# Places of all expert picks made once, eight row buffers, and a third of layer 1's modulations moved ahead of the one-hot vectors

## The reference, cut to what matters

```python
sc = einsum('thsd,hskd->thsk', q, subkeys)      # 8 heads, 2 sides, 128 keys
sv, si = top_k(sc, 16)
best, ci = top_k(sv[:, :, 0, :, None] + sv[:, :, 1, None, :], 16)
idx = i1 * 128 + i2                             # 8 * 16 = 128 picks for each token
act = gelu(x @ u_tab[idx])                      # one number for each pick
out = sum over picks of softmax(best) * act * v_tab[idx]    # rows of 1024
m = silu(c) @ w_mod[layer] + b_mod[layer]       # 48 tiles of 128 modulations
```

## Time and profile before

| | us |
|---|---|
| median of 3 runs (5010.95 to 5015.53) | 5015.15 |
| the profiled execution: its own time | 5005.07 |
| its span in the trace | 5003.3 |
| ACT starts behind layer 0's last input product | 1599.86 |
| the same in layer 1 | 4150.47 |

### The profile page before, as it was taken

One profiled execution on the slowest core, in us unless ns is written; L12 is line 12 of the kernel. 1 busy time (PEld: TensorE's weight loads), 2 busy tenths in 40 slices (PEclk: granted clock), 3 DMA queues, 4 the chain that ended last, 5 costly groups with the idle time before them and its releaser, 6 DMA issues. The chain is left out here.

```text
span 5003.3 us, 77426 instructions
## 1 busy us (share of the span) xinstructions
PE 4526.0 (90%) x27516; PEld 4053.8 (81%) x27516; DVE 3145.1 (63%) x6219; ACT 1177.7 (24%) x1696; POOL 2654.9 (53%) x1462
## 2 busy tenths in 40 slices
PE   7789999999999888888869889999999998999997
PEld 6768999999998666666658679999999997777775
DVE  6962498199994666566643431992799973444444
ACT  2052111132322222222222431110232322222221
POOL 3403455444443777777752124555444436888885
PEclk9889999999999999999988999999999999999998
DMA  5401244377677666666621011444577676666773
GB/s 203 149 9 60 84 120 120 109 154 159 155 162 202 234 244 239 250 236 250 240 76 35 26 47 64 119 119 122 124 159 162 153 172 237 249 251 252 250 253 131
DMA packets 823649, 797.66 MB, mean 159 GB/s; under 512 B 566513, under 2 KB 601041, under 8 KB 822898
## 3 DMA queue, kind: packets, MB, share of 16 engines
q1 hardware_dynamic: 175248, 500.38, 29.8%
q10 hardware_dynamic: 603106, 159.70, 14.8%
q0 software_dynamic: 45056, 134.38, 7.7%
HBM read 640.41 MB, written 153.89 MB: 159 GB/s over the span
## 5 line engine op out<-in xcount | busy, mean ns | idle before, releaser
L498 PE MATMUL acc<-a_hi,w_hi 128*128 128x320 f32 x5296 | 1671.5, 316 | 45.8 <-DVE a_lo L1270 32.3
L500 PE MATMUL acc<-a_hi,w_lo 128*128 128x320 f32 x5296 | 1641.9, 310 | 0.1
L499 PE MATMUL acc<-a_lo,w_hi 128*128 128x320 f32 x5296 | 1641.5, 310 | 0.0
L498 PEld LDWEIGHTS acc<-a_hi,w_hi 128*128 128x128 f32 x5296 | 1000.5, 189 | 51.2 <-issue 35.1
L499 PEld LDWEIGHTS acc<-a_lo,w_hi 128*128 128x128 f32 x5296 | 1001.1, 189 | 1.4 <-issue 0.2
L500 PEld LDWEIGHTS acc<-a_hi,w_lo 128*128 128x128 f32 x5296 | 999.2, 189 | 0.4 <-issue 0.4
L420 POOL TENSOR_TENSOR w_lo<-w_in,w_hi 128x1024 fp32r<-128x1024 f32 (+1 forms) x345 | 891.7, 2585 | 27.7
L436 POOL CAST w_hi<-w_in 128x1024 fp32r<-128x1024 f32 x256 | 306.4, 1197 | 1060.9 <-DMA w_in<-in_u 1060.9
L464 POOL TENSOR_TENSOR w_lo<-w_in,w_hi 128x1024 fp32r<-128x1024 f32 x256 | 698.7, 2729 | 53.8 <-ACT w_hi L1096 49.0
L741 PE MATMUL aux<-p_his,w_hi 128*128 128x512 f32 x1024 | 445.4, 435 | 272.0 <-POOL w_lo L464 149.5
L1505 DVE SCALAR_TENSOR_TENSOR one_b<-iota_b,picks_t 128x384 bf16<-128x384 bf16 x1024 | 633.5, 619 | 0.0
(11 more groups left out here) (244 smaller groups left out, 6265.5 us busy)
## 6 DMA issues: line engine op xcount, KB each, us to landing
w_in<-in_u SPq DMA_DIRECT2D x256, 512.0 KB, 4.0
w_in<-in_v SPq DMA_DIRECT2D x256, 512.0 KB, 5.9
gate_s<-gates ACTq DMA_DIRECT2D x64, 1024.0 KB, 14.0
ag<-act_s SPq DMA_DIRECT2D x256, 256.0 KB, 4.7
ag<-gate_s SPq DMA_DIRECT2D x256, 256.0 KB, 5.3
act_s<-a_out ACTq DMA_DIRECT2D x184, 256.0 KB, 3.6
w_mod_v<-in_w_mod SPq DMA_DIRECT2D x48, 512.0 KB, 3.6
act_s<-tmp ACTq DMA_DIRECT2D x72, 256.0 KB, 3.6
```

What stands on the lines that cost most here:

```text
L498: pe.matmul(out, wh, hi[:, k, n], start=(k == 0), stop=False)
L499: pe.matmul(out, wh, lo[:, k, n], start=False, stop=False)
L500: return pe.matmul(out, wl, hi[:, k, n], start=False, stop=(k == kt - 1))
```

## The change

**Places.** `next_where` is gone. After routing, one cast makes the places of all 128 picks (`where_i`), and POOL waits for them once in each layer. **Buffers.** `found` has eight row buffers; the fetch of row k waits until pick k-8 has been added. The activations land in `pick_act`, a column for each pick, so no fetch of one waits for DVE. POOL's value loop is written out. **Start of the stage.** POOL issues eight row fetches before its first `w_lo`, makes `w_lo` of six chunks, and only then waits for all stored activations (`a_st`) and issues eight activation fetches; before, this wait stood behind the first `w_lo`. From chunk 8 on it issues one row and one activation for each chunk, as before. **Products.** `form` multiplies in place in `ag`, so SP's load of `ag` for chunk n waits for `p_lo` of chunk n-4; SP's order of `ag` and v is swapped, and so is ACT's order of `high_p` and `high_v`. **Modulations.** 16 of the 48 tiles are computed on DVE in layer 0 between the end of the routing (`shifted`) and the exponent, their weights loaded by SP beside the input chunks 48 to 55; the loop computes two tiles for each eight chunks, not three. **Exponent.** ACT takes it eight chunks earlier, in both layers.

```diff
+        MODS_U = 16
+        MODS_AT = range(6 * SPLIT, 7 * SPLIT)
@@ SP
+                if l == 0:
+                    with sp.Fori(0, MODS_AT.start // SPLIT) as i:
+                        for u in range(SPLIT):
+                            load_inputs(u + SPLIT * i, u)
+                    sp.wait_ge(shifted, 1)
+                    for c in MODS_AT:
+                        load_inputs(c, c % SPLIT)
+                        for t in (2 * (c - MODS_AT.start), 2 * (c - MODS_AT.start) + 1):
+                            if t >= 4:
+                                sp.wait_ge(mod_u_used, t - 3)
+                            sp.dma_start(w_mod_u[:, t % 4, :], a["w_mod"][1, t]).then_inc(mod_u_in[t % 4], 16)
...
-                        sp.wait_ge(p_made, NKEY * l + c - 3)
+                        sp.wait_ge(p_lo, NKEY * l + c - 3)
...
                     for u in range(SPLIT):
+                        load_ag(u + SPLIT * i, u)
                         sp.wait_ge(v_done, NKEY * l - SPLIT + u + 1 + SPLIT * i)
                         load_values(u + SPLIT * i, u)
-                        load_ag(u + SPLIT * i, u)
-                        if l == 0 and u < 3:
-                            sp.wait_ge(mod_v_used, u + 1 - 3 + 3 * i)
...
+                        if l == 0 and u in (0, 4):
+                            sp.wait_ge(mod_v_used, 2 * i + u // 4 - 1)
...
@@ POOL
+            def fetch_row(l, k):
+                if PICKS * l + k >= FOUND:
+                    pool.wait_ge(added, PICKS * l + k - FOUND + 1)
+                pool.indirect_dma_start(found[:, k % FOUND, :], None, rows_of_v,
+                                        bass.IndirectOffsetOnAxis(ap=where_i[:, 0, k:k + 1], axis=0))\
+                    .then_inc(found_in[k % FOUND], 16)
+            def values_of(l):
+                pool.wait_ge(where_ready, l + 1)
+                for k in range(2):
+                    pool.wait_ge(gates_out[k], 16 * PIECES * 2 * (NT - 1) * (l + 1))
+                for k in range(FOUND):
+                    fetch_row(l, k)
+                for c in range(NKEY):
+                    if c == 6:
+                        for s in range(4):
+                            pool.wait_ge(a_st[s], 32 * A_ALL[s] * (l + 1))
+                        for k in range(FOUND):
+                            fetch_act(l, k)
+                    slot = (VC[l] + c) % SPLIT
+                    pool.wait_ge(hi_v, NKEY * l + c + 1)
+                    pool.tensor_tensor(w_lo[:, slot, :], landing(slot), w_hi[:, slot, :].bitcast(F),
+                                       ALU.subtract).then_inc(lo_done, 1)
+                    if c >= FOUND:
+                        fetch_row(l, c)
+                        fetch_act(l, c)
@@ ACT
-                with act.Fori(1, EARLY) as i:
+                with act.Fori(1, EARLY - 1) as i:
                     early(i)
                 act.wait_ge(shifted, l + 1)
                 gate_in = picks[:, 2, :, :]
                 act.activation(gate_in, gate_in, ACT.Exp).then_inc(exp_done, 1)
+                early(EARLY - 1)
...
                     for u in range(SPLIT):
+                        high_p(i, u)
                         high_v(i, u)
-                        high_p(i, u)
@@ DVE
+                if l == 0:
+                    for t in range(MODS_U):
+                        dve.wait_ge(mod_u_in[t % 4], 16 * (t // 4 + 1))
...
                 dve.wait_ge(exp_done, l + 1)
...
-                for half in range(2):
-                    next_where(half, 4 * half)
+                dve.tensor_copy(where_i[:], where[:]).then_inc(where_ready, 1)
...
-                    if l == 0 and u in (3, 5, 7):
-                        modulate_v(i, (3, 5, 7).index(u))
+                    if l == 0 and u in (3, 7):
+                        modulate_v(i, u // 4)
```

More of the change, by code:

```diff
@@ L155, in build @@
         w_mod_b = at("w_mod_b", [P, 2, D], work + 44608)
-        w_mod_v = at("w_mod_v", [P, 3, D], work + 40960)
+        w_mod_v = [at(f"w_mod_v{i}", [P, D], act_at + 32768 + 4096 * i) for i in range(2)]
+        w_mod_u = at("w_mod_u", [P, 4, D], work)
+        unread_u = at("unread_u", [P, 2, D], work + 16384)
         unread = at("unread", [P, D], a_out_at)
@@ L229, in build @@
         hi_v, where_ready = sem("hi_v"), sem("where_ready")
-        found_in = [sem(f"found_in{i}") for i in range(4)]
+        found_in = [sem(f"found_in{i}") for i in range(FOUND)]
         act_in = [sem(f"act_in{i}") for i in range(2)]
@@ L479, in _ @@
                 split_loop(l)
-                for k in range(2):
-                    pool.wait_ge(gates_out[k], 16 * PIECES * 2 * (NT - 1) * (l + 1))
-                values_loop(l)
+                values_of(l)
         @block.tensor
@@ L1471, in route @@
                 ins.then_inc(shifted, 1)
+                if l == 0:
+                    for t in range(MODS_U):
+                        dve.wait_ge(mod_u_in[t % 4], 16 * (t // 4 + 1))
+                        wait(dve, mod_u_used, t)
+                        for c in range(2):
+                            ins = dve.tensor_tensor_reduce(out=unread_u[:, c, :], in0=w_mod_u[:, t % 4, :],
+                                                           in1=c_all[:, c, :], scale=1.0, scalar=0.0, op0=ALU.mult,
+                                                           op1=ALU.add, accum_out=mod[:, 1, t, c:c + 1])
+                        ins.then_inc(mod_u_used, 1)
                 dve.wait_ge(exp_done, l + 1)
@@ L1572, in chunk, with body @@
                     low_p(i, u)
[L1574 removed]
+                def body(i):
                     for u in range(SPLIT):
@@ L1577, in body @@
                         chunk(i, u, i - 1 if half else i, half)
-                        if u % 4 == 3 and not (last and u == 7):
-                            dve.wait_ge(added, PICKS * l + u - 3 + SPLIT * i)
-                            next_where(half, 4 + u - 3 + 8 * i if half else 8 + 8 * i)
                 for u in range(4):
@@ L1585, in experts @@
                     chunk(0, u, 0, 0, first=True)
-                dve.wait_ge(added, PICKS * l + 4)
-                next_where(0, 8)
-                with dve.Fori(1, BODIES - 1) as i:
+                with dve.Fori(1, BODIES) as i:
                     body(i)
-                body(BODIES - 1, last=True)
                 parts(BODIES - 1, 1)
```

86 lines of the change are left out of this document (43 added, 43 removed).

## The result

The changed kernel takes 4806.6 us (median of 4, 4797.8 to 4812.1) against 5015.3 for the kernel before: a ratio of 0.958, 95% interval 0.956 to 0.960, or 209 us less, where 169 was forecast. The profiled execution takes 4797.8 us.

The account below looks back on a forecast made before the run. A ring through POOL and DVE, not PE, was taken to bound both value loops. Layer 1's start and loop 69 us, layer 0's 96 and the exponent 4 make 169: 5015 - 169 = 4846 us, range 4785 to 4915.

Parts of the forecast that it names:

- POOL's ring: Value loops: a cycle through POOL and DVE, not PE, sets the period of four chunks, 25.17 and 29.21 us before.
- the new stand: Value loops: POOL would stand 1 to 2 us before a group's second `w_lo`, released by ACT's `high_v`.
- landing: Value loops: from the fourth activation's issue end to `parts`; 2.40 us in layer 1, 3.0 in layer 0.
- Layer 1's period: Layer 1's value loop, four chunks: 23.6 us against 25.17, bounds 22.8 and 25.17.
- Nothing: Value loops: loading `ag` one add later and swapping SP's loads of `ag` and v would cost no time.
- row buffers: Value loops: with eight buffers POOL's 2.46 us wait for DVE's add at a row fetch goes.
- Layer 0's period: Layer 0's value loop, four chunks: 26.7 us against 29.21, bounds 25.3 and 29.21.
- one costs POOL 2.5: Layer 0's value loop: each modulation adds 2.5 us to POOL's work in a group of four chunks.
- The starts: Start of each layer's value stage, to `parts` of chunk 12: 23 us earlier, in layer 0 from 0 to 30.
- The exponent: Routing of both layers: taken eight chunks earlier, it removes PE's 1.99 us wait for `picks_ready`, 4 us together.
- Every `w_lo` collides: Value loops: DVE's adds leave their burst, three more `w_lo` lose 1.4 us each; 5090 us, chance 0.05.
- PE becomes the bound: Value stages: PE's 128 x 5.44 = 696 us sets each stage; about 350 us gained, 4665 us, chance 0.04.

Follow-up runs that it names:

- `high_v` first: The changed kernel with ACT issuing `high_v` before `high_p` of the same chunk; 4698 us, ratio 0.937.
- activations ahead: The changed kernel with each activation fetched four chunks earlier; 4645 us, ratio 0.926.
- the increment back: The changed kernel with four row buffers and `pool.sem_inc(slot_ready, 1)` again between POOL's wait for the add and the row fetch; 4912 us, ratio 0.980.
- four rows without the increment: The changed kernel with four row buffers again and four activations fetched ahead at the start, not eight; 4816 us, ratio 0.960.
- eight with it: The changed kernel, eight row buffers, `pool.sem_inc(slot_ready, 1)` again behind the wait for the add, layer 0's modulations at chunks 1 and 5, not 3 and 7; 4834 us.
- the exponent late: The changed kernel with ACT's exponent behind the last eight early chunks again, as before; 4804 us, ratio 0.959.
- The two four-row kernels: The changed kernel with four row buffers, once with `pool.sem_inc(slot_ready, 1)` again behind the wait for the add (4912 us), once without (4816 us).

## Why the prediction was right, and where it was off

**The direction and the mechanism.** POOL's ring set both loops, the fetch no longer waits, the new stand is where it was put, and without it (`high_v` first, activations ahead) the time falls further. The forecast of -169 came out as -209, inside its range because it was wide and because the errors partly cancel: 50 us too little for layer 0's loop and 8 for the starts, 15 too much for layer 1's and 4 for the exponent. Neither period came where the prediction said it would if right (23 to 24 and 26 to 27 us). The ring has three terms; the measured ones are means of 29 groups:

| us | landing | `parts` to second `w_lo` | from there to the end of the fourth activation's issue | period |
|---|---|---|---|---|
| layer 1 before | 2.41 | 6.27 | 16.49 | 25.17 |
| layer 1 forecast | 2.40 | 4.62 | 16.57 | 23.6 |
| layer 1 after | 3.43 | 4.65 | 16.04 | 24.12 |
| layer 0 before | 4.40 | 5.68 | 19.13 | 29.21 |
| layer 0 forecast | 3.0 | 4.62 | 19.07 | 26.7 |
| layer 0 after | 3.25 | 4.56 | 17.15 | 24.96 |

**Layer 1's period** (23.6 forecast, 24.12 measured). 4.57 us from `parts` to `high_v`'s end was 4.58, and the 16.57 behind it were 16.03. The mis-sized term is the landing: 2.40 forecast, 3.41 in the period above. Taking over a landing from a kernel in which the fourth activation is issued at another moment was the error: it was 2.40 us with the increment back (4333.16 behind the issue that ends at 4330.76) and 3.61 without it, in kernels that differ by that line alone. The row ahead of it in the queue isn't the reason. The traces point at SP's loads. When the fourth activation's issue ends, no load of SP is under way in 28 of 29 groups of layer 1 before (mean landing 2.41 us) and in all 29 with four rows and the increment (2.56). In the changed kernel one is under way in 28 of 29, and the last to land does so 1.7 us later on average (3.43); with `high_v` first 6.0 us later (5.75). In the period above it is this load, issued 5.6 us ahead of the end of the fourth activation's issue and landed 1.5 us behind it:

```profile
4309.12 0.33 SPq L389 DMA_DIRECT2D w_in<-in_v  x1
```

Within these kernels too the later that load lands, the later does the activation (correlation 0.92 and 0.94 in layer 1). No run moved the loads alone, so this is a reading and not shown. It would mean that the prediction's "Nothing" for the order of SP's loads was too quick.

**What "row buffers" bought.** The prediction gave layer 1's gain to the eight buffers. It overlooked that the diff also takes the increment out from behind the wait. Either is enough: four rows without the increment give 23.91 us, eight with it 24.19, neither 25.30. Time by time: 5014 before, 4912 with every edit but these two, 4816 with the increment gone, 4807 with eight rows as well. As the kernel stands, the four extra buffers are worth 10 us of the 209: 18 at the two starts, of which layer 1's loop gives 6 back. With activations ahead they are worth 20 us (4665 to 4645).

**Layer 0's period** (26.7 forecast, 24.96 measured, the largest miss: 123 us and not 73). The failed term is "one costs POOL 2.5". It was read from one group, and that group is an exception: in the other 13 groups with one modulation between chunks 12 and 128 the stretch from row fetch to fourth issue takes 21.8 to 22.0 us and not 22.69, so 1.8 us for the modulation. What sets that group apart is one activation's issue, the only one of 256 above 3.5 us:

```profile
2017.37 3.98 POOL L455 DMA_INDIRECT act_now<-act_p,where_now  x1 [1.96 <-issue]
```

In the changed kernel a modulation at a group's fourth chunk adds 1.11 us to POOL's stretch (17.15 against 16.04 without any) and 0.87 to the period (24.96 against 24.09). Why 1.1 and not 1.8 is not shown. With 0.87 in place of 2.5 the forecast would have been 25.1. Moving 16 modulations is worth 40 us (4847 - 4807). SP, which before waited 123 us in 25 times for a modulation buffer between 1700 and 2450, never does so now, and the long landings that the prediction had seen (5.54 us on average in the groups with two modulations) are gone with it: 1.15 us of each period. That the one comes of the other no run shows by itself.

**The starts** (23 us each). Layer 1: `parts` of chunk 12 at +53.7, forecast +54.3. Layer 0: 30 us, the upper bound given. POOL's first activation in layer 1 starts at +5.8 behind six `w_lo`, against +7.6 assumed:

```profile
4000.78 2.40 POOL L487 TENSOR_TENSOR w_lo<-w_in,w_hi 128x1024 fp32r<-128x1024 f32 x1 [5.21 <-ACT w_hi L1113]
4003.31 1.25 POOL L469 DMA_INDIRECT pick_act<-act_p,where_i  x1
```

**The modulations in the routing** cost nothing, as forecast: they take 65 us of DVE and not 49, end at 939.74, and DVE then stands 41.71 us for the transposed picks. **The exponent** gave 0 and not 4. PE's 1.99 us went, but the stands behind it took their place. Timeline of PE behind the 57th chunk of layer 0, in the changed kernel:

```profile
983.45 1.53 PE L718 MATMUL aux<-ident,picks 128*128 128x128 f32 x8 [1.53 <-ACT picks_t L1075]
...
994.32 1.46 PE L729 MATMUL aux<-one_b,one_a 128*128 128x128 bf16 x12 [5.19 <-DVE one_b L1525]
```

And in the kernel before:

```profile
993.30 1.46 PE L713 MATMUL aux<-one_b,one_a 128*128 128x128 bf16 x12 [4.25 <-DVE one_b L1505]
```

With a stand of 0.37 us between the transposes and these in each kernel, PE stands 7.1 us in all there now, 6.6 before and 6.7 with the exponent late. The failed step is that a stand was counted as gone without asking what PE reaches next: here the one-hot vectors, which wait for the same transposes.

**The rivals.** "Every `w_lo` collides" fell (mean 2.56 us, from 2.73). "PE becomes the bound" is what activations ahead reached: 4645 us, against 4665 worked out.

**The collisions.** The section "Who interferes with whom" of the Trainium skill's page "SBUF — State Buffer" says that the order of issue, not the shape of the operation, decides who is held. The prediction took the 3.80 us of the earlier trace rows for agreement. The two four-row kernels agree in part: the same pair of instructions gave a `w_lo` of 3.77 us or an add of 3.43, as the one or the other came first. But with the increment `w_lo`, from 4339.28, is held for 1.4 us, longer than the add lasts (to 4339.63), while `low_p` and `form`, which start behind it, are not held; and with activations ahead `form` starts 0.32 us ahead of `w_lo` (4197.89 and 4198.21) and is itself held. So the starts that a profile gives do not tell who will be held. The section's inference that a DVE operation with two SBUF inputs leaves descriptor generation alone was said in the prediction to disagree with the trace, and here too a row's issue takes 1.76 us beside such operations (4325.83) and 0.96 elsewhere. That does not refute it: such an issue also takes its places from `where_i` in SBUF, and the rows do not part this read from the generation of descriptors.

## What to carry to other kernels

Read the diff for instructions between a wait and the work that it guards: one that costs nothing while nobody waits can cost 0.5 us at each wake-up, and more where the late engine then loses a collision. The price of a piece of work depends on its place in the ring, and a price read from one group may be that group's own: read several. And when a loop stands once in each period for a small transfer that its own bound engine issues, issue it one period ahead: that, not more buffers, brought the loop to PE's own time.

## What had not been expected of the hardware

A semaphore increment of its own between a wait and an indirect DMA delayed the DMA's start behind the releasing add from 0.28 to 0.81 us, and that half microsecond moved the time by 96 us (1.4 and 1.7 us in each period of layers 1 and 0, and the starts); which of two engines was held changed with it. The landing of a 128-element gather, 2.4 us behind its issue in one kernel and 3.6 in another, took 7.15 us in one group of the run with `high_v` first (issued by 4302.37, `parts` at 4309.52). There SP had issued this load 0.9 us before the issue's end, and it landed 7.3 us behind it:

```profile
4301.47 0.33 SPq L389 DMA_DIRECT2D w_in<-in_v  x1
```
